# Prefetch of input-projection weight blocks, limited to two for the two tiles that wait for the attention buffers

## The reference, cut to what matters

```
x  = x + 0.5 * gate1 * SwiGLU_1(modulate(rmsnorm(x)))          # first FFN
h  = modulate(rmsnorm(x))
dq, dk, dv, gq, gk, gv = split(h @ w_in)                        # input projection
o  = [differential attention (4 heads), grouped-query attention (8 q / 2 kv heads)]
x  = x + gate2 * (o @ w_out)
x  = x + 0.5 * gate3 * SwiGLU_2(modulate(rmsnorm(x)))          # second FFN
y  = rmsnorm(x)
```

## Time and profile before

| | |
|---|---|
| time, median of 3 runs | 3880.34 us (3876.6 to 4100.45) |
| profiled execution, time | 3880.25 us |
| its span, slowest core (core 5) | 3878.7 us |
| spans of the 8 cores | 3856.7 to 3878.7 us |
| mean granted clock of the cores | 0.957 to 0.960 |
| busy on core 5: PE, DVE, ACT, POOL | 90%, 60%, 53%, 3% |
| chain that ended last: PE, DVE, ACT, issue, DMA | 74%, 9%, 7%, 5%, 4% |

### The profile page before, as it was taken

The page is one execution under the profiler, slowest core; times in us unless marked ns, Lnnn a source line. Parts: engine busy times, 40 slices in busy tenths (PEclk is TensorE's granted clock), DMA queues, the critical chain, the costliest instruction groups (busy, mean ns, idle before and its releaser), DMA issues.

```text
span 3878.7 us, 51583 instructions; the slowest of 8 cores (3856.7 to 3878.7 us)
## 1 busy us (share of the span) xinstructions
PE 3498.5 (90%) x15840; PEld 1541.5 (40%) x15840; DVE 2311.9 (60%) x2999; ACT 2043.0 (53%) x2608; POOL 99.8 (3%) x183
## 2 busy tenths in 40 slices
PE   3995899998969698998999999999889999999888
PEld 1442444443434244444344443344334433344333
DVE  5675784543554665564757656566666566576633
ACT  3113323434443443443577667766876678766841
POOL 0000000001010000000000000000000000000000
PEclk7997999999889799999999999999999999999999
DMA  7886776666536167565533423322243232432322
GB/s 218 183 224 214 222 246 181 199 209 168 166 105 189 71 189 216 182 186 213 161 108 140 143 77 125 136 100 83 102 145 110 73 117 80 139 106 82 131 77 92
DMA packets 134842, 572.79 MB, mean 148 GB/s; under 512 B 16848, under 2 KB 22480, under 8 KB 129744
## 3 DMA queue, kind: packets, MB, share of 16 engines
q1 hardware_dynamic: 118304, 491.56, 38.0%
q0 software_dynamic: 16272, 77.93, 9.4%
HBM read 540.40 MB, written 90.51 MB: 163 GB/s over the span
## 4 chain that ended last, share of the span: by engine, by line
PE 74%; DVE 9%; ACT 7%; issue 5%; DMA 4%; DVEq 0%; ACTq 0%; POOL 0%; SPq 0%; POOLq 0%
PE PSA L464 74%; ACT PT L467 3%; DVE RG L470 1%; ACT L467 1%; DVE FIN L477 1%; DVE FIN L484 1%; DVE MT L473 1%; ACT HB L467 1%; DMA DR<-w_dn 1%; DVE NS L470 1%; ACT RG L467 1%; DVE RG L791 1%; DVE PT L473 1%; DMA WR<-s_in 1%; DMA s_vd<-RG 1%
## 5 line engine op out<-in xcount | busy, mean ns | idle before, releaser
L464 PE MATMUL PSA<-HB,WR 128*128 128x512 bf16 x6800 | 1577.9, 387 | 94.0 <-ACT HB L467 33.0
L467 ACT ACTIVATE PT<-PSA 128x1024 bf16<-128x1024 f32 x1184 | 1157.6, 1021 | 418.8 <-PE PSA L464 350.7
L464 PEld LDWEIGHTS PSA<-HB,WR 128*128 128x128 bf16 x6800 | 670.6, 99 | 961.4 <-issue 215.0
L464 PE MATMUL PSA<-QTS,RG 128*128 128x512 bf16 (+1 forms) x2432 | 654.5, 378 | 98.0 <-ACT PT L467 89.8
L464 PE MATMUL PSA<-PT,RG 128*128 128x512 bf16 (+1 forms) x2368 | 645.0, 380 | 9.8 <-ACT PT L467 5.6
L464 PE MATMUL PSA<-HID,DR 128*128 128x512 bf16 x2640 | 594.3, 380 | 13.7 <-DMA DR<-w_dn 13.7
L473 DVE SCALAR_TENSOR_TENSOR TH<-TH,PSA 128x512 f32<-128x512 f32 x352 | 241.0, 685 | 452.6 <-ACT TH L467 450.3
L467 ACT ACTIVATE TH<-PSA 128x512 f32<-128x512 f32 x352 | 209.6, 596 | 568.2 <-PE PSA L464 560.3
L464 PEld LDWEIGHTS PSA<-QTS,RG 128*128 128x128 bf16 (+1 forms) x2432 | 206.1, 98 | 469.2 <-issue 298.6
L464 PEld LDWEIGHTS PSA<-HID,DR 128*128 128x128 bf16 x2640 | 258.5, 98 | 327.6 <-issue 18.1
L467 ACT ACTIVATE SQ<-XB 128x512 f32<-128x512 f32 x226 | 140.8, 627 | 404.2 <-DVE XB L473 339.4
(11 more groups left out here) (91 smaller groups left out, 1601.5 us busy)
## 6 DMA issues: line engine op xcount, KB each, us to landing
WR<-s_gu SPq DMA_DIRECT2D x308, 512.0 KB, 4.3
DR<-s_dn SPq DMA_DIRECT2D x112, 704.0 KB, 4.5
RG<-s_kt SPq DMA_DIRECT2D x64, 576.0 KB, 4.3
WR<-s_in SPq DMA_DIRECT2D x65, 512.0 KB, 5.0
RG<-s_vg SPq DMA_DIRECT2D x32, 864.0 KB, 5.5
PT<-w_ada SPq DMA_DIRECT2D x48, 512.0 KB, 6.2
RG<-s_vd SPq DMA_DIRECT2D x32, 576.0 KB, 4.9
XB<-xs SPq DMA_DIRECT2D x8, 2048.0 KB, 9.4
```

The lines of the kernel that those rows point to most:

```text
L464: return ("pe", (lambda e: e.matmul(out, lhsT, rhs, start=start, stop=stop)), reads, [PK(bank)], c, None, mode)
L467: return ("act", (lambda e: e.activation(out, in_, func, **kw)), reads, writes, 0.18 + n * 0.00082, None)
```

## The change

A loader can be given a gate: after its first two blocks it waits for an event. For p1 and for s4 the event is set when the tile has got `KV`. All other tiles load as before.

```diff
-    def loader(kind, idxs, ring, lock, q, prio):
+    def loader(kind, idxs, ring, lock, q, prio, gate=None):
         yield Get(lock)
-        for i in idxs:
+        for n, i in enumerate(idxs):
+            if gate is not None and n >= 2:
+                yield Get(ev(gate))
...
-    def spawn_loader(kind, idxs, prio):
+    def spawn_loader(kind, idxs, prio, gate=None):
         uid[0] += 1
         q = ("lq", uid[0])
-        S.spawn(loader(kind, idxs, "W", "INL", q, prio), prio)
+        S.spawn(loader(kind, idxs, "W", "INL", q, prio, gate), prio)
...
     # tile_s1
-                       at_dn=lambda: iqs.append(spawn_loader("in", KV_BLK + (Q_BLK if idx >= 4 else []), prio)))
+                       at_dn=lambda: iqs.append(spawn_loader("in", KV_BLK + (Q_BLK if idx >= 4 else []), prio, "kvs4" if idx == 4 else None)))
...
     # tile_s1b
         yield Get("KV")
+        if idx == 4:
+            setf("kvs4")
...
     # tile_prompt
-        yield from ffn(0, [(xb, h)], 0, prio, q, dq, pre=True, at_dn=lambda: iqs.append(spawn_loader("in", KV_BLK + Q_BLK, prio)))
+        yield from ffn(0, [(xb, h)], 0, prio, q, dq, pre=True, at_dn=lambda: iqs.append(spawn_loader("in", KV_BLK + Q_BLK, prio, "kvp1" if idx == 1 else None)))
...
         yield Get("KV")
+        if idx == 1:
+            setf("kvp1")
```

## The result

The changed kernel takes 3927.41 us (median of six runs, 3911.66 to 4412.74). In some executions of any of these kernels one die runs slower at a lower granted clock, and every ratio here, with its 95% interval, compares only executions in which that did not happen. The ratio to the kernel before is 1.009 (1.0053 to 1.0126): slower by about 1%, where 1.1% was forecast (41 us on 3880). A repeat gave the same ratio (first experiment). The eight cores moved unevenly, by 5 us (core 5) to 63 us (core 3); before they lay within 22 us of each other, now within 43. Their mean span went from 3869 to 3907 us. The first scores of the long attention are issued on average at 1936 us instead of 1902 us, so 34 of these 38 us were lost ahead of them, in the first stage.

A forecast was written before the change was run, and what follows sets the result against it. PE was taken as the bound, busy 90% of the span, with 98 us lost in the attentions of p0 and p1. Terms -4 + 8 + 12 + 10 + 15 = +41 us on 3880 gave 3921 us, range 3835 to 3965.

The forecast's parts named there:

- five signs: `in` stops at two; p0 score gap over 100 us; p1 alone; PE gap 9-15 us; `s_in` waits 0-13 us.
- a score group has the hand-over to ACT inside it: In the planner, inner waiting makes a ready score group lose to any FFN group that can start now, whatever its priority.
- Four units are left for after it: p0's attention: four of eight units come after s5's FFN with nothing beside them, 48 us, 38 us lost.
- s5's FFN follows directly: After s4's gate and up part frees `H`, s5's FFN runs directly behind s4's, 76 + 38 us.
- p0's attention, -4: First attention, split around dense FFNs: 46 us lost against 50 before, so -4 us.
- p1's projection, +8: Projection moved behind s5's FFN, beside s6's; seven of nine blocks come just in time: +8 us, bounds 0 and 13.5.
- p1's attention, +12: p1's attention runs alone, with no tile to fill it: 60 us lost against 48, +12 us, bounds 0 and +14.
- The projections of s4 and s5, +10: Both projections run with no FFN beside them, some 11 us lost each instead of about 6: +10 us.
- s5's second norm, +15: s5's second norm comes when `TB` is free and nothing covers it: +15 us.
- The FFN fills the attention: Rival, 20%: all eight p0 units precede s4's down part, p1's attention falls beside s5's FFN; recovers some 60 us, 3820 us.
- The order stays: Rival, 10%: transfers, not buffers, hold the FFN at 1029 us, so the attention starts and ends as before; 3880 us.
- Everything waits in line: Rival, 10%: fewer than two p0 units precede s4's down part, the attention runs alone, projections wait; +88 us, 3968 us.

The follow-up runs named there:

- first experiment: The changed kernel run again without any edit, on one chip with three other kernels: 1.0089 (1.0045 to 1.0132) of the kernel before.
- paced casts: Casts of the second FFN's weights wait until their `HID` block is written; alone on the kernel before 0.9961, with the score groups' switch penalty also off 0.9822 (repeat).
- moved casts: Changed kernel with two weight casts behind p1's store of x done only an eighth there, the rest at s6's projection: 1.004 (1.0007 to 1.0073) of the kernel before.

## Why the prediction was right, and where it was not

**The time and the frame.** 3921 us were forecast and 3927 measured. The starvation that it removes was real and is gone: in the timeline above s4's FFN no longer stops. That it would bring nothing, since the attention gets in only where the FFN has nothing to offer, is what happened: p0's attention stands behind a down part of 176 matmuls, for half of its units. Of the five signs that were named only the first came as written (`in` issues stop at two). The gap among p0's scores is 71 us behind one down part, not over 100 us behind two, p1's attention has FFN matmuls in it, and on core 3 neither the norm's gap nor a wait at p1's third block is there.

**Why the attention loses.** The step "a score group has the hand-over to ACT inside it" is wrong; it is the planned mode switch of 0.13 us, and taking it off gave 0.988. The observation (ready for 83 us, not issued) carried the forecast, and it doesn't depend on which it is. The switch was a line away in the code I quoted from, and would have pointed to the cure at once.

**How many units, and where.** "Four units are left for after it": four is right (of the sixteen score groups eight are issued ahead of the down part and eight behind it). "s5's FFN follows directly" is wrong: the rest came after s4's down part, not after s5's FFN. s5 gets its `H` only when s4's gate and up part ends, and the matmul of its norm was then planned behind the dense down part, at 1150.89 us. So p1's projection ran beside s5's gate and up part, and not behind s5's FFN and beside s6's. s5's norm and the attention's finish shared DVE. In order of time on DVE, core 3:

```profile
1157.17 1.42 DVE L473 SCALAR_TENSOR_TENSOR MT<-XB,GS,RSTD 128x512 f32<-128x512 f32 x2 [0.97 <-ACT RSTD L467]
1159.84 3.36 DVE L484 RECIPROCAL FIN<-PSA 128x512 f32<-128x512 f32 x1 [1.25 <-PE PSA L464]
...
1182.32 3.36 DVE L484 RECIPROCAL FIN<-PSA 128x512 f32<-128x512 f32 x1
...
1186.39 0.75 DVE L473 SCALAR_TENSOR_TENSOR MT<-XB,GS,RSTD 128x512 f32<-128x512 f32 x1
```

From the first `MT` to the last, eight steps of 0.75 us take 30 us, since three reciprocals and their like stand between.

**The terms.** *p0's attention, -4.* Lost are: 26.2 us from the end of the run at 1019.55 to the first scores at 1045.76, less 32 x 0.217 = 7 us of matmuls, so 19; some 9 of 45 us in the first part; and 42 - 10 (attention) - 3.5 (FFN) - 1 (the norm's matmul) = 27 in the second. That is 55 us against 50: +5 and not -4. What I had mis-sized is the first half, for which I took 8 us lost in all: it lost 28, of which 19 are this stall (14.5 us of waiting, and slower matmuls). The second half lost 27 and not 38. *p1's projection, +8.* No wait for an input block there on core 3; 9.75 us for gate and up blocks instead, in two waits at 1297 and 1310 us. Its upper bound rested on a wrong reading as well: the 13.5 us at 1492 were not a wait "behind a load of x". SP issues no load of x from 1440 to 1500 us on that core; POOL issues a store of x and three casts at 1466 us, and with paced casts the same place has no wait. *p1's attention, +12.* It was not alone: once s6's norm was through, s6's FFN came in from 1407 us. In the 102 us of the stretch above are some 168 matmuls of 512 columns (36 us) and 20 us of attention, so 46 us are lost, against 48. *The projections of s4 and s5, +10, and s5's second norm, +15.* These followed from s5's FFN being done early, and that didn't happen. What came in their place is in the list of waits: DVE steps of FFNs, +14.2 us, norms +6.9, transfers +21.6 (of which p1's stretch and p0's are the 24.2 on `s_gu`).

So that the sum was right within 6 us is luck; errors met: +9 and +2 on p0 and the projection, -14 on p1's attention, -25 on what was to follow. What the terms name comes to 13 us on core 3 (5 + 10 - 2), where the sum had 41. The rest is in no term: 33 of the 46 us that core 3 took longer up to the long attention, and by the mean span, 38 us, some 25. Only the sign, the frame and the split of p0's units are confirmed. The forecast's own range, 3880 to 3955, was also wider than what was named for it: by the same terms the low end comes to some 3892 (-8, -9.5, -12) and the high end to some 3934 (+5.5, +2, +5).

**The rivals.** *The FFN fills the attention*, at 20%, is where the reading by the Trainium skill led (Perfetto Trace Analysis, Optimization Strategy: repeated gaps can mean too little buffer space). Here four more buffers for the FFN made it slower, 1.009, two more made it a little faster, 0.9962, and an order with no more buffers made it faster still, 0.988. So buffer space is one cause among others, as the page's "can" allows, but the rival, by which four free buffers recover 60 us, is refuted. *The order stays* fell with the timeline, which has p0's scores cut in two. *Everything waits in line*: four units of p0 were ahead of the down part, not fewer than two, as its condition asked.

**The cores.** Core 3 lost 63 us and core 5 only 5, but much of that spread lies ahead of the gate. p1's down part, in which the gated loader starts, begins at 959.8 us on core 3 after and 947.8 before, and on core 5 at 943.9 after and 962.5 before; the mean of the eight cores hardly moved (952.7, 953.9). From there to the long attention core 3 lost 46 us, core 5 20 us and the mean 33 us. Of the 26 us that are left between the two, some 13 are transfers: between 1000 and 2000 us PE waited 39 us for them on core 3 (17 before) and 24 us on core 5 (15 before).

**Left open.** Why the start of p1's down part moves by up to 19 us on a core between the two executions, although nothing ahead of it was changed. The 14 us more on DVE steps and the slower matmuls were read and not taken away by an experiment. The changed kernel was not run with paced casts, so the 0.4% that is left with the moved casts is put down to the order by reading alone.

## What to carry to other kernels

A buffer that is full may be what lets another stream in. Before freeing it, look how long the waiting work had been ready and what it was passed over for; if it waits for the planner and not for data, change the order first. In a kernel whose order a planner writes, its constants are part of the program: a switch cost of 0.13 us held back an attention for 83 us. And a pacing key only paces if it is written after the point where it is read; four transfers that leave in one burst show it.

## What the runs showed of the hardware that was not expected

With one store of 2 MB and four casts (1 MB read and 0.5 MB written each) under way, a 512 KB block took 25.8 us to land (median of six, core 3). At the like place with the store and two casts it took 9.4 us (core 3 of the kernel before), and 5.0 us in the median of all input blocks. The waits that the burst caused differed among cores that run the same program: 8 to 16 us near 1030 us.
